# Two sides of a head's decay levels in one VectorE instruction each, and the third token tile's values on both halves of the array

## The chip, the cores and the metric

The kernel runs on one core of a Trainium2 chip. The metric is device time in microseconds, the median of the timed runs.

## What is computed

One inference step of one layer over T = 320 frames: 256 of a prompt and 64 of a running stream, D_MODEL = 1024. In order: an entry LayerNorm, one combined projection, branch A (a gated linear recurrence, HGRN2, with 8 heads of 128x128 state), branch B (a depthwise convolution), their gated mix, a LayerNorm, a mixture of 16 experts with top-2 routing, a last LayerNorm. All in float32. What matters here is branch A of one head:

```
S_t = diag(f_t) S_{t-1} + k_t v_t^T ;  o_t = S_t^T q_t
b     = cumsum(log f)                                     # per block of frames
attn  = sum_d q[t,d] k[s,d] exp(b[t,d] - b[s,d])          # for s <= t
o     = attn v + (q exp(b)) S
S_new = exp(b_last) S + (k exp(b_last - b))^T v
```

## The kernel before

The frames are held as columns: a head's q, k and running sums are 128x320 (channel x frame), in three token tiles of 128, 128 and 64 frames (`TILES`).

**Levels.** exp(b[t] - b[s]) is split at an anchor between s and t, so that no exponent is positive. For half sizes hs = 64, 32, 16, 8, 4, 2, 1 (`LV`, seven levels) a stretch of 2*hs frames has a key half in front of the anchor and a query half behind it. `X[b]` holds for each level, at offset `XO[lv]`, anchor - b in the key halves and b - anchor in the query halves: 256 columns for the first level, 320 for each of the others, 2176 in all. GpSimd writes the key halves (`key_decay`, line 1515) and VectorE the query halves (`level_decay`, line 1681), each in seven instructions of 128x160 (128x128 for the first level). ScalarE takes the exponential of all of `X[b]` in one instruction (line 1214). Then GpSimd multiplies the key halves by k (`key_side`, line 1529) and VectorE the query halves by q (`query_side`, line 1694), seven instructions each again. TensorE multiplies the halves of each level, in 64x64 blocks, into the banks of `levels`; VectorE masks the blocks (1717, 1724) and folds seven into four (1728), and GpSimd adds these up in three instructions (`level_sums`, 1541 to 1543) into `hAS`, the attention weights that `prev_out` takes.

**The order of the work.** A turn handles one head and the rests of the two before it. Each engine has its own program, written out by hand, and works it in order; semaphores tie them together. There are eight turns (`head_turn`); six are in loops of two turns. Per turn:

- VectorE: `forget_in` (log f, and at line 1672 the scan that makes the running sums `hb`), mask and fold of the head before, `level_decay`, `pprev_out` (1746), `w_low` for the next head (1641), `prev_final` (1737, 1739), `query_side`, `carry_side` (1704 to 1708), `w_low` again.
- ScalarE: `forget` (1180 to 1186), key exponential, copies, then `level_exp` (1214), `tile_exp` (1222, 1224), `w_high` (1133), `v_copy` (1206 and 1207), the square of the output (1257), two DMA issues for the states (1263), and `forget` of the next head.
- TensorE: forget projection, sum of squares, levels, transposes of the keys (line 632), query projection, states, values (`cur_v`), output of the head before.
- GpSimd: `key_decay`, `level_sums` of the head before, `key_side`.

The value projection has frames as rows: for each token tile eight matmuls (one for each 128 of the 1024 inputs) with the frames as the stationary operand (128 or 64 columns) and 128 columns of weights moving. The third tile has 64 frames and takes 64 columns of the array.

After the turns come the convolution's taps on VectorE beside the gate projections on TensorE (to about 295 us), then branch outputs, mix and router, and then the experts, for which 200 MB of weights are loaded.

Of the kernel before, what the change touches and what calls it, by code (L numbers as in the profile page):

```python
# [124 lines left out]
def build(nc, a, o):  # L125
    with ExitStack() as ctx:
# [51 lines left out]
        def carve(first, *sizes):  # L178
            out, at = [], first
            for n in sizes:  # L180
# [20 lines left out]
        (hq, hk, hV, he, hw, hls, hb, heb, hqeb, hkde, hkT, hAM, hAS, hSA, hosq, hrs, hebl, _, hSst, hSo) = carve(  # L201
            0, 2 * T, 2 * T, 384, T, T, T, T, T, T, T, 384, 3 * LW, 384, P, T, T, 4, 892, 2 * P, 2 * P)
# [65 lines left out]
        names = ("f_done q_done v_done ls_ready w_ready k_ready b_ready dr_ready dl_ready E_ready q_sb ac_ready "  # L268
                 "kde_ready xr_ready xk_ready a_done am_ready as_ready qeb_ready kdec_ready kT_done kT_sb s_done sa_sb o_done "
                 "osq_ready rms_done rstd_ready rstd_exp o_out so_ready so_stored hc_dve hp_dve hc_act hp_act hc_pool hp_pool fold_ready v_sb round")  # L270
# [270 lines left out]
        def _(pe):  # L541
# [51 lines left out]

            def cur_v(i, b, first, after_rms=False):
                pe.wait_ge(wh_in[b], i * 48 + (16, 48)[b])
                if not first:
                    pe.wait_ge(h["v_sb"], 2 * i + b)
                if after_rms:
                    pe.wait_ge(h["rstd_ready"], 2 * i + b - 1)
                value_tile(b, 0)  # L600
                value_tile(b, 1)
                value_tile(b, 2).then_inc(h["v_done"], 1)

            def levels(i, b, first):

                n1 = 2 * i + b
                pe.wait_ge(h["xr_ready"], n1 + 1)
                pe.wait_ge(h["xk_ready"], n1 + 1)
                if not first:
                    pe.wait_ge(h["am_ready"], 2 * n1)  # L610
                    pe.wait_ge(h["ac_ready"], n1)
                for t, (t0, n) in enumerate(TILES):
                    bank = LEVEL_BANKS[t]
                    for lv in range(1, 8):
                        for m in range(n // BLK):
                            s0 = t0 + BLK * m
                            if lv < 7:
                                lo = ro = X[b][:, XO[lv] + s0:XO[lv] + s0 + BLK]
                            else:
                                lo, ro = hk[:, b, s0:s0 + BLK], hq[:, b, s0:s0 + BLK]  # L620
                            last = mm(ps[BLK * m:BLK * m + BLK, bank, (lv - 1) * BLK:lv * BLK], lo, ro, True, True)
                    if t < 2:
                        last = mm(ps[0:BLK, bank, LW:LW + BLK], X[b][:, t0:t0 + BLK], X[b][:, t0 + BLK:t0 + 2 * BLK], True, True)
                    if t:
                        last.then_inc(h["a_done"], 1)

            def prev_kT(i, b, first):
                pe.wait_ge(h["kdec_ready"], 2 * i + b + 1)
                if not first:
                    pe.wait_ge(h["so_ready"], 2 * i + b)  # L630
                for t, (t0, n) in enumerate(TILES):
                    last = pe.transpose(ps[0:n, 7, t * P:t * P + P], hkde[:, t0:t0 + n], ident)
                last.then_inc(h["kT_done"], 1)

            def prev_states(i, b):
                n1 = 2 * i + b
                pe.wait_ge(h["kT_sb"], n1 + 1)
                pe.wait_ge(h["v_sb"], n1 + 1)
                for t, (t0, n) in enumerate(TILES):
                    last = mm(ps[:, 7, t * P:t * P + P], hkT[0:n, t, :], hV[0:n, t, :], True, True)  # L640
                last.then_inc(h["s_done"], 1)

            def prev_out(i, b, first):
# [7 lines left out]
                pe.wait_ge(h["as_ready"], 2 * n1 + 2)  # L651
# [5 lines left out]
                mm(ps[:, 6, 256:320], hV[0:64, 2, :], hAS[0:64, 2, 0:64], False, True).then_inc(h["o_done"], 1)  # L657
# [441 lines left out]
        def _(act):  # L1099
# [22 lines left out]
            cc = Chain(act, h["hc_act"], 6)  # L1122
            pc = Chain(act, h["hp_act"], 1)
# [77 lines left out]
            def v_copy(i, b, first):  # L1201
# [4 lines left out]
                cc(act.activation(hV[:, 0:2, :], ps[:, 3, 0:256].rearrange("p (t n) -> p t n", t=2), ACT.Copy))  # L1206
                signal(act, act.activation(hV[0:64, 2, :], ps[0:64, 3, 256:384], ACT.Copy), h["v_sb"], n + 1)

            def level_exp(i, b):
# [3 lines left out]
                act.wait_ge(h["dl_ready"], n + 1)  # L1213
# [13 lines left out]
            def prev_states(i, b, first):  # L1227
# [4 lines left out]
                pc.turn(n)  # L1232
                pc(act.activation(hkT[:, 0:2, :], ps[:, 7, 0:256].rearrange("p (t n) -> p t n", t=2), ACT.Copy))
                signal(act, act.activation(hkT[0:64, 2, :], ps[0:64, 7, 256:384], ACT.Copy), h["kT_sb"], n + 1)
# [264 lines left out]
        def _(pool):  # L1499
# [3 lines left out]
            cc = Chain(pool, h["hc_pool"], 12)  # L1503
            pc = Chain(pool, h["hp_pool"], 1)

            def key_decay(i, b):

                n = 2 * i + b
                cc.turn(n)
                pool.wait_ge(h["b_ready"], n + 1)  # L1510
                for lv, hs in enumerate(LV):
                    w = SEQ if lv == 0 else T
                    xv = X[b][:, XO[lv]:XO[lv] + w].rearrange("p (m s) -> p m s", s=2 * hs)[:, :, 0:hs]
                    bv = hb[:, 0:w].rearrange("p (m s) -> p m s", s=2 * hs)
                    ins = pool.tensor_tensor(xv, bv[:, :, hs - 1:hs].to_broadcast([P, w // (2 * hs), hs]), bv[:, :, 0:hs], ALU.subtract)  # L1515
                    if lv < 6:
                        cc(ins)
                signal(pool, ins, h["dl_ready"], n + 1)

            def key_side(i, b):  # L1520

                n = 2 * i + b
                pool.wait_ge(h["E_ready"], n + 1)
                pool.wait_ge(h["k_ready"], n + 1)
                for lv, hs in enumerate(LV):
                    w = SEQ if lv == 0 else T
                    xv = X[b][:, XO[lv]:XO[lv] + w].rearrange("p (m s) -> p m s", s=2 * hs)[:, :, 0:hs]
                    kv = hk[:, b, 0:w].rearrange("p (m s) -> p m s", s=2 * hs)[:, :, 0:hs]
                    ins = pool.tensor_tensor(xv, xv, kv, ALU.mult)  # L1529
                    if lv < 6:  # L1530
                        cc(ins)
                signal(pool, ins, h["xk_ready"], n + 1)
                cc.end()

            def level_sums(i, b, first):
# [6 lines left out]
                signal(pool, pool.tensor_tensor(hAS[BLK:P, 0:2, BLK:P], hAM[BLK:P, 0:2, 0:BLK], hAM[BLK:P, 0:2, BLK:2 * BLK], ALU.add), h["as_ready"], 2 * n + 1)  # L1542
                signal(pool, pool.tensor_tensor(hAS[0:BLK, :, 0:BLK], hAM[0:BLK, :, 0:BLK], hAM[0:BLK, :, BLK:2 * BLK], ALU.add), h["as_ready"], 2 * n + 2)
# [10 lines left out]
            head_turn((0, 0), None)  # L1554
            head_turn((0, 1), (0, 0), True)
# [3 lines left out]
            with pool.Fori(1, 4) as i:  # L1559
                head_turn((i, 0), (i - 1, 1))  # L1560
                head_turn((i, 1), (i, 0))


            head_turn(None, (3, 1))

            pool.wait_ge(tlo_ready, 2 * NG)
            for c in range(1, CT):
                pool.wait_ge(conv_done, c + 1)
                ins = pool.tensor_tensor(csum, cT[:, 0, :] if c == 1 else csum, cT[:, c, :], ALU.add)
                if c < CT - 1:  # L1570
                    signal(pool, ins, h["hc_pool"], 12 * HEADS + c)
# [4 lines left out]
        def _(dve):  # L1576
# [80 lines left out]
            cc = Chain(dve, h["hc_dve"], 15)  # L1657
            pc = Chain(dve, h["hp_dve"], 1)

            def forget_in(i, b, first):  # L1660
# [8 lines left out]
                if not (first and b == 0):  # L1669
                    dve.wait_ge(h["kde_ready"], 3 * n)  # L1670
                    dve.wait_ge(h["dl_ready"], n)
                signal(dve, dve.tensor_tensor_scan(hb, reset, hls, 0.0, ALU.mult, ALU.add), h["b_ready"], n + 1)  # L1672

            def level_decay(i, b):

                n = 2 * i + b
                for lv, hs in enumerate(LV):
                    w = SEQ if lv == 0 else T
                    xv = X[b][:, XO[lv]:XO[lv] + w].rearrange("p (m s) -> p m s", s=2 * hs)
                    bv = hb[:, 0:w].rearrange("p (m s) -> p m s", s=2 * hs)  # L1680
                    ins = dve.tensor_tensor(xv[:, :, hs:2 * hs], bv[:, :, hs:2 * hs], bv[:, :, hs - 1:hs].to_broadcast([P, w // (2 * hs), hs]), ALU.subtract)  # L1681
# [4 lines left out]
            def query_side(i, b):  # L1686
                n = 2 * i + b
                dve.wait_ge(h["E_ready"], n + 1)
                dve.wait_ge(h["q_sb"], n + 1)
                for lv, hs in enumerate(LV):  # L1690
                    w = SEQ if lv == 0 else T
                    xv = X[b][:, XO[lv]:XO[lv] + w].rearrange("p (m s) -> p m s", s=2 * hs)[:, :, hs:2 * hs]
                    qv = hq[:, b, 0:w].rearrange("p (m s) -> p m s", s=2 * hs)[:, :, hs:2 * hs]
                    ins = dve.tensor_tensor(xv, xv, qv, ALU.mult)  # L1694
# [16 lines left out]
            def level_mask(i, b, first):  # L1711
                n = 2 * i + b
                dve.wait_ge(h["a_done"], 2 * n + 1)
                if not first:
                    dve.wait_ge(h["as_ready"], 2 * n - 1)
# [3 lines left out]
            def last_mask(i, b, first):  # L1719
                n = 2 * i + b  # L1720
                dve.wait_ge(h["a_done"], 2 * n + 2)
                if not first:
                    dve.wait_ge(h["as_ready"], 2 * n)
# [24 lines left out]
            def head_turn(cur, nxt, prev, pprev, first=False, first_prev=False):  # L1748
# [16 lines left out]
                query_side(*cur)  # L1765
# [496 lines left out]
```

## Time and profile before

| | |
|---|---|
| median of 3 runs | 856.8 us (855.72 to 857.4) |
| span of the profiled execution | 854.3 us |
| PE busy | 812.5 us, 95% |
| DVE busy | 423.0 us, 50%, 706 instructions |
| ACT busy | 239.4 us, 28%, 378 instructions |
| POOL (GpSimd) busy | 84.0 us, 10%, 146 instructions |
| HBM traffic | 293 GB/s over the span |

The span is that of one execution taken by the hardware profiler, from the first to the last instruction; it has no other time of its own on the page. The timed median is 2.5 us over it. The page's busy shares are means over stages with different limits.

### The profile page before, as it was taken

How to read it: one execution, taken by the hardware profiler on the slowest of the kernel's cores; microseconds unless marked ns; L12 is line 12 of the kernel's file. 1: busy time of each engine (PE TensorE's matmuls, PEld its weight loads, DVE VectorE, ACT ScalarE, POOL GpSimd, SP SyncE). 2: the span in 40 equal slices, each digit the busy share in tenths (PEclk: the TensorE clock that was granted, in tenths of full speed). 3: DMA queues.
4: the chain of work that ended last, by engine and by line, in shares of the span. 5: the costliest groups of instructions: out<-in, count | busy, mean ns of one | idle time of the engine just before them, and what ended most of it. 6: DMA issues, size and time to landing. Idle time of an engine off the chain costs nothing.

```text
span 854.3 us, 12979 instructions
## 1 busy us (share of the span) xinstructions
PE 812.5 (95%) x5068; PEld 525.6 (62%) x5068; DVE 423.0 (50%) x706; ACT 239.4 (28%) x378; POOL 84.0 (10%) x146
## 2 busy tenths in 40 slices
PE   4999999999999999999999999999999999999892
PEld 2988888999999976576353453534435344352261
DVE  6788888988999993786010201202012021120137
ACT  5656666564454426102102010000100001000011
POOL 1354445530000100000000000000000000000000
PEclk9999999999999999999999999999999999999996
DMA  8422222234444844578999999999999999999991
GB/s 315 171 84 85 83 83 83 107 125 161 148 148 147 320 172 143 229 289 340 425 411 407 429 427 430 424 427 427 428 423 427 427 428 428 428 422 426 429 390 64
DMA packets 33883, 251.16 MB, mean 294 GB/s; under 512 B 4974, under 2 KB 8430, under 8 KB 21674
## 3 DMA queue, kind: packets, MB, share of 16 engines
q1 hardware_dynamic: 31296, 249.18, 71.9%
q10 hardware_dynamic: 2538, 1.32, 0.5%
q8 instruction: 33, 0.54, 0.2%
q14 instruction: 16, 0.13, 0.0%
HBM read 247.99 MB, written 2.48 MB: 293 GB/s over the span
## 4 chain that ended last, share of the span: by engine, by line
PE 57%; DVE 21%; DMA 9%; ACT 9%; issue 2%; ACTq 1%; DVEq 0%; SPq 0%
PE ps L543 56%; DMA ring<-in_w_up_e 8%; DVE ar L1803 5%; DVE ring L1681 4%; DVE split_t L1810 3%; ACT ring L1214 2%; ACT ar L1224 1%; DVE ar L1717 1%; ACT split_w L1133 1%; DVE ar L1728 1%; PE ps L942 1%; DVE ar L1672 1%; ACTq L1263 1%; ACT ar L1186 1%; DMA ring<-in_w_in 1%
## 5 line engine op out<-in xcount | busy, mean ns | idle before, releaser
L543 PE MATMUL ps<-ring,ar 128*64 128x512 f32 (+1 forms) x976 | 202.0, 567 | 1.1 <-DMA ring<-in_w_up_e 1.1
L543 PE MATMUL ps<-ring,xT 128*64 128x512 f32 (+2 forms) x848 | 149.5, 451 | 4.6 <-DMA ring<-in_w_gate_e 3.0
L543 PEld LDWEIGHTS ps<-ring,ar 128*64 128x64 f32 x976 | 68.0, 137 | 120.3 <-issue 112.5
L543 PEld LDWEIGHTS ps<-ring,xT 128*64 128x64 f32 (+1 forms) x848 | 75.2, 153 | 71.7 <-issue 62.7
L543 PE MATMUL ps<-split_x,split_t 128*128 128x320 f32 x672 | 101.0, 310 | 0.5 <-DVE split_t L1810 0.5
L543 PEld LDWEIGHTS ps<-split_x,split_t 128*128 128x128 f32 x672 | 98.6, 188 | 2.5 <-issue 0.8
L2113 DVE TENSOR_TENSOR ar<-ar,ps 128x512 f32<-128x512 f32 (+1 forms) x42 | 28.8, 685 | 134.5 <-PE ps L543 132.7
L543 PE MATMUL ps<-split_x,split_w 128*128 128x320 f32 x480 | 80.7, 324 | 3.3 <-ACT split_x L1165 1.0
L543 PEld LDWEIGHTS ps<-split_x,split_w 128*128 128x128 f32 x480 | 74.1, 196 | 6.5 <-ACT split_x L1168 2.1
L1803 DVE SCALAR_TENSOR_TENSOR ar<-ar,params 128x350 f32<-128x350 f32 x116 | 68.7, 592 | 4.1
L543 PE MATMUL ps<-ar 128*64 128x512 f32 (+7 forms) x424 | 66.7, 342 | 2.9 <-DVE mid L1746 2.9
L2080 DVE SCALAR_TENSOR_TENSOR out_lo<-ps,ar,out_hi 128x1024 fp32r<-128x1024 f32 x7 | 9.0, 1284 | 104.6 <-ACT out_hi L1434 104.6
L543 PEld LDWEIGHTS ps<-ar 128*64 128x64 f32 (+3 forms) x424 | 39.6, 152 | 25.4 <-issue 22.9
L543 PEld LDWEIGHTS ps<-ar,mid 128*128 128x128 f32 x384 | 43.6, 192 | 8.3 <-issue 7.3
L543 PE MATMUL ps<-ar,mid 128*128 128x128 f32 x384 | 45.5, 278 | 0.2 <-DVE ar L2068 0.2
L543 PE MATMUL ps<-mid,ring 128*128 128x320 f32 x128 | 34.9, 432 | 0.0
L1515 POOL TENSOR_TENSOR ring<-ar 128x160 f32<-128x160 f32 (+1 forms) x56 | 28.2, 503 | 63.3 <-DVE ar L1672 59.5
L1434 ACT ACTIVATE out_hi<-ps,ar 128x1024 fp32r<-128x1024 f32 x7 | 7.8, 1114 | 94.2 <-PE ps L543 94.2
L2094 DVE TENSOR_TENSOR ar<-ar,ps 128x1024 f32<-128x1024 f32 x7 | 8.5, 1221 | 51.7 <-PE ps L543 51.7
L1417 ACT ACTIVATE ar<-ps 128x1024 f32<-128x1024 f32 x8 | 8.2, 1026 | 88.5 <-PE ps L543 88.4
L1529 POOL TENSOR_TENSOR ring<-ring,ar 128x160 f32<-128x160 f32 (+1 forms) x56 | 30.4, 542 | 25.1 <-ACT ring L1214 16.0
L1694 DVE TENSOR_TENSOR ring<-ring,ar 128x160 f32<-128x160 f32 (+1 forms) x56 | 30.4, 543 | 2.1 <-ACT ring L1214 0.2
(233 smaller groups left out, 860.9 us busy)
## 6 DMA issues: line engine op xcount, KB each, us to landing
ring<-in_w_gate_e SPq DMA_DIRECT2D x29, 2048.0 KB, 21.0
ring<-in_w_up_e SPq DMA_DIRECT2D x29, 2048.0 KB, 17.4
ring<-in_w_down_e SPq DMA_DIRECT2D x22, 2048.0 KB, 17.3
ring<-in_w_in SPq DMA_DIRECT2D x56, 512.0 KB, 4.5
ar<-in_w_down_e SPq DMA_DIRECT2D x4, 1792.0 KB, 18.7
ring<-in_w_down_end SPq DMA_DIRECT2D x3, 2048.0 KB, 35.3
ar<-in_w_up_e SPq DMA_DIRECT2D x3, 1792.0 KB, 14.5
ring<-in_w_o_a SPq DMA_DIRECT2D x8, 512.0 KB, 5.4
```

What stands on the lines that cost most here:

```text
L543: return pe.matmul(out, lhsT, rhs, start=start, stop=stop)
L942: last = pe.transpose(ps[:, k // 4, (k % 4) * P:(k % 4) * P + P], eh[:, k * P:k * P + P], ident)
L1133: signal(act, act.activation(piece(wh, q), sh[:, b, q].rearrange("p k n -> p (k n)"), ACT.Copy), whi_ready, 2 * n + q + 1)
L1214: signal(act, act.activation(X[b], X[b], ACT.Exp), h["E_ready"], n + 1)
L1515: ins = pool.tensor_tensor(xv, bv[:, :, hs - 1:hs].to_broadcast([P, w // (2 * hs), hs]), bv[:, :, 0:hs], ALU.subtract)
L1529: ins = pool.tensor_tensor(xv, xv, kv, ALU.mult)
L1681: ins = dve.tensor_tensor(xv[:, :, hs:2 * hs], bv[:, :, hs:2 * hs], bv[:, :, hs - 1:hs].to_broadcast([P, w // (2 * hs), hs]), ALU.subtract)
L1694: ins = dve.tensor_tensor(xv, xv, qv, ALU.mult)
L1803: vc(dve.scalar_tensor_tensor(acc, uc[:, c, j:j + CW], vt[:, c, j:j + 1], acc, ALU.mult, ALU.add))
L1810: signal(dve, dve.tensor_tensor(t_lo[1 - b][q][1], stl[:, b, 8 * q:8 * q + 8].rearrange("p k n -> p (k n)"), t_hi[1 - b][q][0], ALU.subtract),
L2080: signal(dve, dve.scalar_tensor_tensor(out_lo[:, :], ps[:, 6:8, :].rearrange("p b n -> p (b n)"), gs, hiF, ALU.mult, ALU.subtract), e["eos ...
L2113: signal(dve, dve.tensor_tensor(yv, yv, ps[0:c, 4 + j % 2, :], ALU.add), e["y_added"], 6 * n + j + 1 + 6 * late)
```

## The change

Four edits.

1. VectorE writes both sides of a level in one instruction. It needs -b beside b, so the negated sums `hnb` are laid in front of `hb`, by one new instruction after the scan; `both_sums` is a view whose first half lies in `hnb` (key halves) and whose second half, T + hs further, lies in `hb` (query halves), and `anchors` is the anchor of each. The multiplication does the same with `hk` laid in front of `hq` (`key_query`). The seven instructions of `level_decay` and the seven of the multiplication now have 320 columns (256 for the first level); GpSimd's fourteen are gone with the semaphores around them, and it keeps `level_sums`.
2. The values of the third token tile are computed in two halves of the array: even inputs k into rows 0 to 63, odd ones into rows 64 to 127 of PSUM. The two partial sums are never added: the keys and attention weights that meet them are held twice, in both halves.
3. For that the third tile's key transpose becomes two matmuls against the identity (one for each half), and `level_sums` has a fourth instruction, which writes the third tile's weights into rows 64 to 127.
4. ScalarE's `v_copy` and the copy of the transposed keys are one instruction of 128x384 each, in place of 128x256 and 64x128.

```diff
+        (hk, hq, hV, he, hw, hls, hnb, hb, heb, ...) = carve(...)
+        NB_AT = 4 * T + 384 + 3 * T
+        def key_query(b, hs, w):
+            v = ar[:, b * T:b * T + 2 * (2 * T + hs)].rearrange("p (j t) -> p j t", j=2)[:, :, 0:w]
+            return v.rearrange("p j (m s) -> p m j s", s=2 * hs)[:, :, :, 0:hs]
+        def both_sums(hs, w):
+            v = ar[:, NB_AT:NB_AT + 2 * (T + hs)].rearrange("p (j t) -> p j t", j=2)[:, :, 0:w]
+            return v.rearrange("p j (m s) -> p m j s", s=2 * hs)[:, :, :, 0:hs]
+        def anchors(hs, w):
+            v = ar[:, NB_AT:NB_AT + 2 * T].rearrange("p (j t) -> p j t", j=2)[:, :, 0:w]
+            return v.rearrange("p j (m s) -> p m j s", s=2 * hs)[:, :, :, hs - 1:hs].to_broadcast([P, w // (2 * hs), 2, hs])
...
+            def value_halves(b):
+                for k in range(KT):
+                    side = 64 * (k % 2)
+                    last = mm(ps[side:side + 64, 3, 2 * P:3 * P], xT[:, k, SEQ:T], sh[:, b, 3, k, :], k < 2, k >= KT - 2)
+                return last
...
-                value_tile(b, 2).then_inc(h["v_done"], 1)
+                value_halves(b).then_inc(h["v_done"], 1)
...
-                for t, (t0, n) in enumerate(TILES):
-                    last = pe.transpose(ps[0:n, 7, t * P:t * P + P], hkde[:, t0:t0 + n], ident)
+                for t in range(2):
+                    pe.transpose(ps[:, 7, t * P:t * P + P], hkde[:, t * P:t * P + P], ident)
+                for side in (0, 64):
+                    last = mm(ps[side:side + 64, 7, 2 * P:3 * P], hkde[:, SEQ:T], ident, True, True)
...
-                cc(act.activation(hV[:, 0:2, :], ps[:, 3, 0:256].rearrange("p (t n) -> p t n", t=2), ACT.Copy))
-                signal(act, act.activation(hV[0:64, 2, :], ps[0:64, 3, 256:384], ACT.Copy), h["v_sb"], n + 1)
+                signal(act, act.activation(hV, ps[:, 3, 0:384].rearrange("p (t n) -> p t n", t=3), ACT.Copy), h["v_sb"], n + 1)
...
-            def head_turn(cur, prev, first_prev=False):
-                if cur:
-                    key_decay(*cur)
-                if prev:
-                    level_sums(*prev, first_prev)
-                if cur:
-                    key_side(*cur)
...
+                signal(pool, pool.tensor_tensor(hAS[BLK:P, 2, 0:BLK], hAM[0:BLK, 2, 0:BLK], hAM[0:BLK, 2, BLK:2 * BLK], ALU.add), h["as_ready"], 3 * n + 3)
...
                 signal(dve, dve.tensor_tensor_scan(hb, reset, hls, 0.0, ALU.mult, ALU.add), h["b_ready"], n + 1)
+                cc(dve.tensor_scalar(hnb, hb, -1.0, None, ALU.mult))
...
-                    ins = dve.tensor_tensor(xv[:, :, hs:2 * hs], bv[:, :, hs:2 * hs], bv[:, :, hs - 1:hs].to_broadcast([P, w // (2 * hs), hs]), ALU.subtract)
+                    ins = dve.tensor_tensor(xv, both_sums(hs, w), anchors(hs, w), ALU.subtract)
...
-                    ins = dve.tensor_tensor(xv, xv, qv, ALU.mult)
+                    ins = dve.tensor_tensor(xv, xv, key_query(b, hs, w), ALU.mult)
```

## Rows read from the trace of the kernel before

**Rows 1.** Page: shares of the chain that ended last, by engine.
```profile
PE 57%; DVE 21%; DMA 9%; ACT 9%; issue 2%; ACTq 1%; DVEq 0%; SPq 0%
```
**Rows 2.** Busy time by stretch: window, us, engines, clock, DMA share, GB/s.
```profile
65.00:165.00 100.00, 96.52 (x958) 89.27 (x958) 87.17 (x147) 63.73 (x117) 47.30 (x85) 1.00 0.28 94
200.00:295.00 95.00, 94.71 (x638) 93.19 (x636) 88.92 (x136) 48.34 (x59) 0.00 (x0) 1.00 0.49 177
295.00:854.00 559.00, 535.38 (x2758) 264.29 (x2757) 166.18 (x288) 68.13 (x103) 3.06 (x3) 0.99 0.90 373
```
**Rows 3.** Chain of waits: start, us, what; scans of the third and eighth turns.
```profile
65.30 0.84 DVE ar L1672
...
164.63 0.84 DVE ar L1672
```
**Rows 4.** Timeline of DVE: start, us, what; second, sixth and eighth turns.
```profile
46.57 1.09 DVE L1717 TENSOR_TENSOR ar<-ps,mid 128x896 f32<-128x896 f32 x1 [0.49 <-PE ps L543]
...
128.89 0.76 DVE L1728 TENSOR_TENSOR ar<-ar 128x576 f32<-128x576 f32 x1
129.68 4.15 DVE L1681 TENSOR_TENSOR ring<-ar 128x128 f32<-128x128 f32 x7
...
136.94 3.90 DVE L1694 TENSOR_TENSOR ring<-ring,ar 128x128 f32<-128x128 f32 x7
...
143.91 0.49 DVE L1664 SCALAR_TENSOR_TENSOR ar<-ps,ar 128x320 f32<-128x320 f32 x1 [0.31 <-ACT ar L1186]
...
167.26 0.88 DVE L1728 TENSOR_TENSOR ar<-ar 128x576 f32<-128x576 f32 x1
168.18 4.15 DVE L1681 TENSOR_TENSOR ring<-ar 128x128 f32<-128x128 f32 x7
```
**Rows 5.** Timeline of ACT, 133 to 142 us.
```profile
133.91 2.02 ACT L1214 ACTIVATE ring<-ring 128x2176 f32<-128x2176 f32 x1 [4.64 <-DVE ring L1681]
...
138.81 0.38 ACT L1206 ACTIVATE ar<-ps 128x256 f32<-128x256 f32 x1
139.22 0.27 ACT L1207 ACTIVATE ar<-ps 64x128 f32<-64x128 f32 x1
139.53 0.44 ACT L1257 ACTIVATE ar<-ps 128x320 f32<-128x320 f32 x1
...
141.19 0.44 ACT L1180 ACTIVATE ar<-ps 128x320 f32<-128x320 f32 x1 [1.22 <-issue]
```
**Rows 6.** Timeline of PE: two stretches of levels, values, output.
```profile
121.04 0.92 PE L543 MATMUL ps<-ring 128*64 128x64 f32 x24
...
122.84 0.98 PE L543 MATMUL ps<-ring 128*64 128x64 f32 x14
...
128.73 5.73 PE L543 MATMUL ps<-ring,xT 128*128 128x128 f32 x48
134.89 1.44 PE L543 MATMUL ps<-ar 128*128 128x128 f32 x10 [0.43 <-DVE mid L1746]
```
**Rows 7.** Groups of DVE by line and shape: busy, mean ns.
```profile
L1707 DVE TENSOR_TENSOR ar<-ar 128x320 f32<-128x320 f32 x8 | 3.9, 492 | 0.3
...
L1883 DVE TENSOR_SCALAR ar<-cst 128x128 f32<-128x128 f32 x1 | 0.2, 228 | 0.0
L1969 DVE TENSOR_SCALAR ar<-cst 128x12 f32<-128x12 f32 x1 | 0.2, 166 | 0.0
```
**Rows 8.** Chain of waits, last instructions of the sixth turn's level_decay.
```profile
131.24 1.05 DVE ring L1681
...
132.31 0.51 DVE ring L1681
...
132.84 0.64 DVE ring L1681
...
133.50 0.34 DVE ring L1681
```
**Rows 9.** Timeline of POOL, the first of that turn's level sums.
```profile
131.10 0.99 POOL L1541 TENSOR_TENSOR ar<-ar 128x384 f32<-128x384 f32 x1
```

More of the change, by code:

```diff
@@ L199, in build @@
         sgu = sgu_f.rearrange("p (b n) -> p b n", b=2)
-        (hq, hk, hV, he, hw, hls, hb, heb, hqeb, hkde, hkT, hAM, hAS, hSA, hosq, hrs, hebl, _, hSst, hSo) = carve(
-            0, 2 * T, 2 * T, 384, T, T, T, T, T, T, T, 384, 3 * LW, 384, P, T, T, 4, 892, 2 * P, 2 * P)
+        (hk, hq, hV, he, hw, hls, hnb, hb, heb, hqeb, hkde, hkT, hAM, hAS, hSA, hosq, hrs, hebl, _, hSst, hSo) = carve(
+            0, 2 * T, 2 * T, 384, T, T, T, T, T, T, T, T, 384, 3 * LW, 384, P, T, T, 4, 892 - T, 2 * P, 2 * P)
+        NB_AT = 4 * T + 384 + 3 * T
[8 more added lines that the diff above has]
+            return v.rearrange("p j (m s) -> p m j s", s=2 * hs)[:, :, :, hs - 1:hs].to_broadcast([P, w // (2 * hs), 2, hs])
         two = lambda v: v.rearrange("p (b n) -> p b n", b=2)
@@ L267, in build @@
         st_in = [sem(f"st_in{b}") for b in range(2)]
-        names = ("f_done q_done v_done ls_ready w_ready k_ready b_ready dr_ready dl_ready E_ready q_sb ac_ready "
-                 "kde_ready xr_ready xk_ready a_done am_ready as_ready qeb_ready kdec_ready kT_done kT_sb s_done sa_sb o_done "
-                 "osq_ready rms_done rstd_ready rstd_exp o_out so_ready so_stored hc_dve hp_dve hc_act hp_act hc_pool hp_pool fold_ready v_sb round")
+        names = ("f_done q_done v_done ls_ready w_ready k_ready b_ready dr_ready E_ready q_sb ac_ready "
+                 "kde_ready xr_ready a_done am_ready as_ready qeb_ready kdec_ready kT_done kT_sb s_done sa_sb o_done "
+                 "osq_ready rms_done rstd_ready rstd_exp o_out so_ready so_stored hc_dve hp_dve hc_act hc_pool hp_pool fold_ready v_sb round")
         h = {n: sem(n) for n in names.split()}
@@ L639, in prev_states @@
                 for t, (t0, n) in enumerate(TILES):
-                    last = mm(ps[:, 7, t * P:t * P + P], hkT[0:n, t, :], hV[0:n, t, :], True, True)
+                    last = mm(ps[:, 7, t * P:t * P + P], hkT[:, t, :], hV[:, t, :], True, True)
                 last.then_inc(h["s_done"], 1)
@@ L650, in prev_out @@
                 pe.wait_ge(h["sa_sb"], n1 + 1)
-                pe.wait_ge(h["as_ready"], 2 * n1 + 2)
+                pe.wait_ge(h["as_ready"], 3 * n1 + 3)
                 pe.wait_ge(h["ac_ready"], n1 + 1)
@@ L1231, in prev_states @@
                     act.wait_ge(h["s_done"], n)
-                pc.turn(n)
-                pc(act.activation(hkT[:, 0:2, :], ps[:, 7, 0:256].rearrange("p (t n) -> p t n", t=2), ACT.Copy))
-                signal(act, act.activation(hkT[0:64, 2, :], ps[0:64, 7, 256:384], ACT.Copy), h["kT_sb"], n + 1)
+                signal(act, act.activation(hkT, ps[:, 7, 0:384].rearrange("p (t n) -> p t n", t=3), ACT.Copy), h["kT_sb"], n + 1)
             def prev_cross(i, b, first):
@@ L1502, in _ @@
             signal(pool, pool.tensor_tensor(piece(wl, 0), sh[:, 0, 0].rearrange("p k n -> p (k n)"), piece(whF, 0), ALU.subtract), wlo_ready, 1)
-            cc = Chain(pool, h["hc_pool"], 12)
             pc = Chain(pool, h["hp_pool"], 1)
[L1506 to L1533, printed above, removed]
             def level_sums(i, b, first):
@@ L1541, in level_sums @@
                 pc(pool.tensor_tensor(hAM[:, :, 0:2 * BLK], hAM[:, :, 0:2 * BLK], hAM[:, :, 2 * BLK:4 * BLK], ALU.add))
-                signal(pool, pool.tensor_tensor(hAS[BLK:P, 0:2, BLK:P], hAM[BLK:P, 0:2, 0:BLK], hAM[BLK:P, 0:2, BLK:2 * BLK], ALU.add), h["as_ready"], 2 * n + 1)
-                signal(pool, pool.tensor_tensor(hAS[0:BLK, :, 0:BLK], hAM[0:BLK, :, 0:BLK], hAM[0:BLK, :, BLK:2 * BLK], ALU.add), h["as_ready"], 2 * n + 2)
+                signal(pool, pool.tensor_tensor(hAS[BLK:P, 0:2, BLK:P], hAM[BLK:P, 0:2, 0:BLK], hAM[BLK:P, 0:2, BLK:2 * BLK], ALU.add), h["as_ready"], 3 * n + 1)
+                signal(pool, pool.tensor_tensor(hAS[0:BLK, :, 0:BLK], hAM[0:BLK, :, 0:BLK], hAM[0:BLK, :, BLK:2 * BLK], ALU.add), h["as_ready"], 3 * n + 2)
+                signal(pool, pool.tensor_tensor(hAS[BLK:P, 2, 0:BLK], hAM[0:BLK, 2, 0:BLK], hAM[0:BLK, 2, BLK:2 * BLK], ALU.add), h["as_ready"], 3 * n + 3)
                 pc.end()
-            def head_turn(cur, prev, first_prev=False):
-                if cur:
-                    key_decay(*cur)
-                if prev:
-                    level_sums(*prev, first_prev)
-                if cur:
-                    key_side(*cur)
-            head_turn((0, 0), None)
-            head_turn((0, 1), (0, 0), True)
+            level_sums(0, 0, True)
             pool.wait_ge(router_in, 32)
@@ L1559, in _ @@
             with pool.Fori(1, 4) as i:
-                head_turn((i, 0), (i - 1, 1))
-                head_turn((i, 1), (i, 0))
-            head_turn(None, (3, 1))
+                level_sums(i - 1, 1, False)
+                level_sums(i, 0, False)
+            level_sums(3, 1, False)
             pool.wait_ge(tlo_ready, 2 * NG)
@@ L1570, in _ @@
                 if c < CT - 1:
-                    signal(pool, ins, h["hc_pool"], 12 * HEADS + c)
+                    signal(pool, ins, h["hc_pool"], c)
             ins.then_inc(csum_ready, 1)
@@ L1656, in _ @@
             signal(dve, dve.memset(hrs, 0.0), h["o_out"], 1)
-            cc = Chain(dve, h["hc_dve"], 15)
+            cc = Chain(dve, h["hc_dve"], 16)
             pc = Chain(dve, h["hp_dve"], 1)
@@ L1684, in level_decay, with both_sides @@
                 signal(dve, ins, h["dr_ready"], n + 1)
-            def query_side(i, b):
+            def both_sides(i, b):
                 n = 2 * i + b
@@ L1714, in level_mask @@
                 if not first:
-                    dve.wait_ge(h["as_ready"], 2 * n - 1)
+                    dve.wait_ge(h["as_ready"], 3 * n)
                 wide = mask.rearrange("p (o n) -> p o n", o=1).to_broadcast([P, 2, LW])
@@ L1722, in last_mask @@
                 if not first:
[L1723 removed]
+                    dve.wait_ge(h["as_ready"], 3 * n)
                 signal(dve, dve.tensor_tensor(hAM[0:BLK, 2, :], ps[0:BLK, LEVEL_BANKS[2], 0:LW], mask[0:BLK, :], ALU.mult), h["am_ready"], 2 * n + 2)
@@ L1764, in head_turn @@
                     w_low(*nxt, 1)
-                query_side(*cur)
+                both_sides(*cur)
                 carry_side(*cur, first)
```

15 lines of the change are left out of this document (5 added, 10 removed).

## The prediction

> **What bounds the kernel now.** I read the shares of the chain first [rows 1]: TensorE carries 57% and VectorE 21%, so the bound changes by stage. Busy time by stretch shows where [rows 2]. From 295 us on the experts keep TensorE (535 of 559 us) and the DMAs (0.90) full and VectorE idle; nothing of the change lies there. From 200 to 295 us VectorE and TensorE are both nearly full, with no instruction touched. The change lies in the eight head turns, 31 to 180 us: TensorE is 97% busy, VectorE 87%, GpSimd 47%, so which engine ends a turn has to be read from waits.
>
> A turn is 19.9 us: five lie between the scans at 65.30 and 164.63 us [rows 3]. In the timeline of one turn [rows 4] VectorE ends `level_decay` at 133.83; ScalarE, idle for 4.64 us until then, starts its exponential at 133.91 [rows 5] and works without a hole through `tile_exp`, `w_high`, `v_copy`, the square, the DMA issues and `forget` of the next head, for whose last result VectorE waits 0.31 us at 143.91 [rows 4]. Then VectorE again: `forget_in`, scan, masks, fold, `level_decay`. That is the loop: 9.8 us on VectorE, 10 us on ScalarE. Beside it VectorE alone comes within 0.31 us of a full turn, and TensorE within 0.43 us, waiting for `pprev_out` (line 1746), which stands right behind `level_decay` [rows 6]. So a time counts in full if it lies between w_ready and the end of `level_decay` on VectorE or between `level_exp` and `forget` on ScalarE. The rest of VectorE counts once its small slack is used, and TensorE's saving only if the loop gets shorter.
>
> **The change, part by part.**
>
> *The negated sums.* One instruction between scan and mask, on the loop. A tensor_scalar with a constant took 0.166 us for 12 columns and 0.228 for 128 [rows 7], 0.53 ns for a column, so 0.33 for 320, and 0.03 for the gap: +0.37 a turn. Bounds: 0.23 (128 columns) and 0.49, what a tensor_tensor of 320 columns takes.
>
> *level_decay, alone.* 320 columns of tensor_tensor are 0.49 us [rows 7] and 160 are 0.34 [rows 8] (the last one there), so 256 are 0.43. One of 0.43, six of 0.49 and the gaps of 0.02 make 3.5 to 3.6; I take 3.57. Alone, seven of the old ones would make 2.5. The doubled instructions are cheaper than two, but the other half of that work was on GpSimd.
>
> *level_decay beside level_sums.* What hid it before was partly paid for: old instructions took 1.05, 0.51 and 0.64 us where one with nothing beside it took 0.34 [rows 8]. The first of them meets GpSimd's sum of 128x384 at 131.10 [rows 9]: VectorE is held for 1.05 - 0.34 = 0.71, then 0.17 and 0.30 by the two small sums. This doesn't go away. `level_sums` is released by the fold, right in front of `level_decay`, and with `key_decay` gone GpSimd is free to start it at once, so all sums fall into the seven instructions: 0.71 + 0.17 + 0.30, and about 0.10 for the new fourth one (64x64, an estimate from the 0.17 of 64x128) = 1.28. The block of seven becomes 3.57 + 1.28 = 4.85. The fold is freed from `key_decay` and takes 0.76. From the fold's start to the end of `level_decay` before: 4.94 at 128.89 and 5.07 at 167.26 [rows 4], the smallest and largest of the seven turns that have a fold, mean 5.00. After: 0.79 + 4.85 = 5.64. So +0.64 a turn. Bounds: -0.64 if no sum holds VectorE, +0.92 if the wide sum holds it for its whole 0.99 [rows 9] in place of 0.71.
>
> The Trainium skill ("SBUF — State Buffer", Who interferes with whom) says that a VectorE instruction with two SBUF inputs and a GpSimd instruction that reads SBUF exclude each other, the later one blocked for the whole of the other. Here the 0.99 us sum held VectorE 0.71, not 0.99. By the whole duration the block would be larger by 0.28 us a turn, some 2 us in all, about 864.5; the sum goes by the measured hold.
>
> *The multiplication.* 3.90 before [rows 4], with GpSimd beside it throughout; 3.57 with GpSimd idle: -0.33, on VectorE's side branch. All of VectorE's turn grows by 0.37 + 0.64 - 0.33 = 0.68, the loop by more (below), so VectorE's slack goes from 0.31 to about 0.4 and it stays behind the loop. GpSimd's fourteen instructions were not on the loop, but for the first turn.
>
> *v_copy.* 0.38 + 0.27 and a gap of 0.03 each [rows 5] become one of 384 columns. 256 columns took 0.38 and 320 took 0.44, so 384 take 0.49, with the gap 0.51 for 0.72: -0.21, on the loop. The same saving on the transposed keys lies in ScalarE's 4.64 us of idle time: nothing.
>
> *Third value tile.* 24 matmuls took 5.73 us [rows 6], so eight are 1.9. In the levels 12 matmuls that alternate between the halves of the array took some 0.75 us (121.04 to the next group), seven of the lone third tile 0.82 (122.84 on): 62 against 117 ns each. At that ratio the eight take 1.0, so TensorE saves 0.9 a turn. It waited 0.43 for `pprev_out` already; the saving makes that wait longer. Worth nothing (at most 0.9 a turn, were TensorE the bound). The two identity matmuls in place of a transpose add some 0.1, hidden likewise, but for the last turn: behind it TensorE works without a hole for 17 us, so +0.1 once.
>
> *Sum.* A turn: +0.37 + 0.64 - 0.21 = +0.80; six turns (third to eighth): 4.8. The second turn's mask waits 0.49 for TensorE's levels [rows 4], which hides its own negation; but that TensorE work starts behind the first turn's `level_decay` and low parts, later by the first turn's negation: +0.4, + 0.64 - 0.21 = 0.83. With the 0.1 at the end 5.7. The following stages are full and start that much later. 854.3 + 5.7 = 860.0 for the span; the median of the runs stands 2.5 over the profiled span, so **862.5 us**.
>
> **The rivals.**
>
> *The stride costs.* For hs = 1 the new views jump between `hnb` and `hb` at every column. No row of before shows VectorE reading so. Were its data phase twice as long, one of seven would take 0.33 more: eight turns of `level_decay` are +2.6, and the multiplications another 0.33 on the side branch, still inside its slack. Time: about 865. For hs = 2 the same would double it, 867.7, the upper end. The Trainium skill ("SBUF — State Buffer", Door 1: The DMA port swizzle) states that an access pays for each change of a 16-byte line unless two accesses fall into it; by that hs = 1 pays and hs = 2 doesn't. No run here shows it.
>
> *GpSimd doesn't get in (the other side).* Place: the gap of 0.02 us between two VectorE instructions. If GpSimd's sums wait until the seven are through, `level_decay` and fold take 3.57 + 0.79 = 4.36, so 0.64 less, and a turn changes by 0.37 - 0.64 - 0.21 = -0.48: seven turns are -3.3, time about 853.5. It decides from the point where the four sums hold VectorE less than 0.8 us a turn in place of 1.28. Against it: in every turn before, GpSimd's wide sum did get in (1.05 us at 131.24). For it: the sums could also be shorter in their hold once nothing else queues.
>
> *The halves don't overlap* (the change doesn't do what it says): TensorE's eight matmuls keep their 1.9 us. TensorE's own turn stays 19.5 us against a loop of 20.7: same 862.5.
>
> *The delay is absorbed.* If the experts' stage were set by transfers that don't start later, the 5.7 us would come back: 857. Against it: loads wait for places that earlier stages free.
>
> **How the numbers follow.** The main case (with the halves either way) 0.52, stride 0.25, GpSimd locked out or the holds small 0.14, absorbed 0.06, something worse 0.03. Likeliest 862.5; its own range 860 to 864.5 from the bounds of negation and holds. The range to give is 857 to 867: it leaves out the faster case and little above. Within 0.2% means 855.1 to 858.5, about what a measurement of this kernel can tell from no change. Slower: main, stride and the worse case, 0.80; same: 0.07; faster: 0.13.
>
> **What would show it.** In the changed trace: a tensor_scalar of 0.33 us behind each scan; `level_decay` of about 4.85 us, in which the second instruction takes about 1.2, and of 3.57 in the first turn; the multiplication 3.57 with equal instructions of 0.49; one ScalarE copy of 0.49; scans 20.7 us apart in place of 19.9; TensorE's wait for `pprev_out` above 1 us; TensorE's values 4.8 us in place of 5.7. An hs = 1 instruction (the seventh) of 0.8 is the stride case. A second instruction of 0.49 is the case of GpSimd locked out. Scans under 20 us apart with the rows as forecast would mean that I have the wrong loop.

## The result, and the profile after

| | before | after |
|---|---|---|
| median | 856.56 us (4 runs, 855.72 to 857.4) | 862.53 us (4 runs, 860.67 to 866.9) |
| ratio | | 1.0083, 95% interval 1.0066 to 1.010 |
| profiled execution: span, granted clock | 854.3 us, 0.992 | 865.0 us, 0.981 (time 866.9) |
| GpSimd busy | 84.0 us | 31.7 us |
| third to eighth scan, per turn | 19.87 us | 20.95 us |

The change makes the kernel 0.8% slower, some 6 us, clear of the noise; the forecast was 862.5. The four executions are of two kinds: two of 860.7 us with a mean granted clock of 0.987 and 0.989, and 864.3 and 866.9 at 0.981 to 0.982. The profiled one is the slowest of them. (Time and span of one execution differ by 1.9 us: 866.9 and 865.0 here, and 856.2 in a later execution of the kernel before whose span was 854.3 too. So 1.9 us lie around a span, not 2.5.)

The VectorE and GpSimd timelines of the sixth turn after, against [rows 4, 9]:

```profile
132.44 0.82 DVE L1650 TENSOR_TENSOR_SCAN ar<-cst,ar 128x320 f32<-128x320 f32 x1
133.30 0.33 DVE L1651 TENSOR_SCALAR ar<-ar 128x320 f32<-128x320 f32 x1
...
135.75 0.76 DVE L1706 TENSOR_TENSOR ar<-ar 128x576 f32<-128x576 f32 x1
136.54 4.75 DVE L1659 TENSOR_TENSOR ring<-ar 128x256 f32<-128x256 f32 x7
```
```profile
136.59 1.23 POOL L1530 TENSOR_TENSOR ar<-ar 128x384 f32<-128x384 f32 x1 [19.14 <-DVE ar L1706]
...
139.37 0.45 POOL L1533 TENSOR_TENSOR ar<-ar 64x64 f32<-64x64 f32 x1
```

`level_decay` has grown from 4.15 to 4.75 us. The chain of waits shows its seven instructions one by one, against [rows 8]:

```profile
136.54 0.44 DVE ring L1659
...
137.00 1.18 DVE ring L1659
...
138.21 0.65 DVE ring L1659
...
138.87 0.78 DVE ring L1659
...
139.67 0.50 DVE ring L1659
...
140.20 0.50 DVE ring L1659
...
140.73 0.58 DVE ring L1659
```

An instruction with nothing beside it takes 0.50 (the fifth and sixth). The second is held 0.68 us by the wide sum, the third 0.15, the fourth 0.28, the fifth not at all. The wide sum's 1.23 us start 0.41 before the second instruction does, so only its last 0.82 us lie beside it. The last, hs = 1, takes 0.08 more than its neighbours.

These holds are not new. Before, the sums held the same stretch of VectorE for 0.71 + 0.17 + 0.30 us [rows 8], and its first instructions were longer too while GpSimd's `key_decay` ran beside them (0.54 and 0.51 us for 160 columns, against 0.34 alone):

```profile
129.68 0.44 DVE ring L1681
...
130.14 0.54 DVE ring L1681
...
130.70 0.51 DVE ring L1681
```

So of the 4.15 us before some 2.5 were its own work and 1.65 lay in holding; of the 4.75 after, 3.66 are its own work (e2_late_sums, below) and 1.09 holding. The block grew by the half that GpSimd had done, not by the sums.

The multiplication (line 1672), the joined copy (line 1229) and the negation (line 1651) by groups:

```profile
L1672 DVE TENSOR_TENSOR ring<-ring,ar 128x320 f32<-128x320 f32 x48 | 24.3, 506 | 1.6
...
L1651 DVE TENSOR_SCALAR ar<-ar 128x320 f32<-128x320 f32 x8 | 2.6, 327 | 0.3
```
```profile
L1229 ACT ACTIVATE ar<-ps 128x384 f32<-128x384 f32 x8 | 3.9, 492 | 0.3
```

What the forecast did not have is in TensorE's timeline of the turn before this one, against [rows 6]. The first two lines are an undisturbed turn, the output matmuls and the forget projection:

```profile
99.10 1.30 PE L559 MATMUL ps<-ar 128*128 128x128 f32 x10 [1.54 <-DVE mid L1724]
100.21 3.76 PE L559 MATMUL ps<-split_x,split_w 128*128 128x320 f32 x24
...
112.77 4.76 PE L559 MATMUL ps<-ring,xT 128*128 128x128 f32 x48
120.09 2.37 PE L559 MATMUL ps<-ar 128*128 128x128 f32 x10 [2.56 <-DVE mid L1724]
122.22 5.62 PE L559 MATMUL ps<-split_x,split_w 128*128 128x320 f32 x24
```

The values take 4.76 us in place of 5.73, then TensorE waits 2.56 us for `pprev_out`, and behind that wait the output matmuls (ten records) take 2.37 us in place of 1.30 (1.44 before) and the forget projection 5.62 in place of 3.76: the granted clock is at its lower level, 0.50 or half of the full one, from 120 to 126 us. `forget` on ScalarE then waits for TensorE, and VectorE's wait for `forget` is 2.16 us. This turn took 22.45 us. The same happened, for a shorter time, behind a wait of 2.49 us (output matmuls 1.91, forget projection 4.77), and not behind those of 1.54 and 1.53. A third drop lies ahead of the third scan and so outside the mean of the turns: behind a wait of 2.18 us the second turn's forget and query projections take 8.85 us, against 7.31 before.

```profile
37.31 8.85 PE ps L559 x48
```

### The profile page after: what moved, and what is told of

It reads as the page before. It is cut to its first block, busy times and chain, and to the rows that moved or that the text cites. A ratio compares the mean times of both kernels' runs of the same rounds, so it can differ in the third digit from the quotient of the medians.

```text
span 865.0 us, 12835 instructions
## 1 busy us (share of the span) xinstructions
PE 812.2 (94%) x5092; PEld 525.3 (61%) x5092; DVE 426.4 (49%) x714; ACT 236.6 (27%) x362; POOL 31.7 (4%) x42
## 3 DMA queue, kind: packets, MB, share of 16 engines
q10 hardware_dynamic: 2538, 1.32, 0.5%
## 4 chain that ended last, share of the span: by engine, by line
PE 60%; DVE 22%; DMA 8%; ACT 7%; issue 2%; ACTq 0%; DVEq 0%
PE ps L559 58%; DMA ring<-in_w_up_e 8%; DVE ar L1781 6%; DVE ring L1659 4%; DVE split_t L1788 3%; ACT ring L1235 1%; DVE ar L1695 1%; PE ps L966 1%; ACT ar L1245 1%; DVE ar L1650 1%; DVE ar L1706 1%; ACT split_w L1156 1%; ACT ar L1209 1%; DVE ring L1569 1%; DVE ar L1702 1%
## 5 line engine op out<-in xcount | busy, mean ns | idle before, releaser
L559 PE MATMUL ps<-ring,xT 128*64 128x512 f32 (+2 forms) x848 | 141.8, 451 | 4.6 <-DMA ring<-in_w_gate_e 3.0
L559 PEld LDWEIGHTS ps<-ring,xT 128*64 128x64 f32 (+1 forms) x848 | 68.3, 153 | 70.8 <-issue 62.6
L559 PE MATMUL ps<-split_x,split_w 128*128 128x320 f32 x480 | 85.0, 336 | 6.1 <-DVE split_w L1620 3.5
L559 PEld LDWEIGHTS ps<-split_x,split_w 128*128 128x128 f32 x480 | 78.5, 207 | 10.2 <-DVE split_w L1620 3.9
L559 PE MATMUL ps<-ar 128*64 128x512 f32 (+5 forms) x424 | 65.7, 345 | 11.0 <-DVE mid L1724 11.0
L559 PEld LDWEIGHTS ps<-ar 128*64 128x64 f32 (+2 forms) x424 | 40.0, 158 | 32.1 <-issue 31.1
L1659 DVE TENSOR_TENSOR ring<-ar 128x320 f32<-128x320 f32 (+1 forms) x56 | 35.4, 632 | 1.9
L1175 ACT ACTIVATE split_t<-ring 128x1024 fp32r<-128x1024 f32 x24 | 25.5, 1061 | 20.3 <-DMA ring<-in_w_in 11.6
L559 PEld LDWEIGHTS ps<-mid,ring 128*128 128x128 f32 x128 | 24.3, 190 | 10.1
```

What stands on the lines that cost most here:

```text
L559: return pe.matmul(out, lhsT, rhs, start=start, stop=stop)
L1175: signal(act, act.activation(t_hi[1 - b][q][1], stl[:, b, 8 * q:8 * q + 8].rearrange("p k n -> p (k n)"), ACT.Copy), thi_ready, 2 * n + q + 1)
L1659: ins = dve.tensor_tensor(xv, both_sums(hs, w), anchors(hs, w), ALU.subtract)
```

## The experiments

One table first. Times are medians. The runs were spread over several chips of the same kind; each ratio is to the kernel before on the same chip, whose median was between 855.7 and 856.4, with its 95% interval. "Turn" is a fifth of the time from the third to the eighth scan in the profile.

| kernel | median us (lowest to highest) | ratio to before | turn us |
|---|---|---|---|
| before (time beside e1 to e4, turn of the profile before) | 855.74 | | 19.87 |
| changed, again (a1_after) | 865.01 (863.33 to 866.22) | 1.0093 (1.0078 to 1.0109) | 20.94 |
| e1_series | 863.66 (862.37 to 863.68) | 1.0087 (1.0074 to 1.0100) | 20.47 |
| e2_late_sums | 880.46 (877.0 to 881.59) | 1.0275 (1.0255 to 1.0295) | 23.39 |
| e3_mult_only | 855.86 (854.49 to 857.13) | 0.9998 (0.9989 to 1.0007) | 19.66 |
| e4_halves_only | 856.24 (854.07 to 860.58) | 1.0003 (0.9989 to 1.0017) | 19.72 |
| e5_no_negation | not comparable | | 20.33 |
| e6_short_sum | not comparable | | 19.83 |
| e7_filler | 862.75 (862.52 to 863.85) | 1.0075 (1.0061 to 1.0088) | 20.50 |
| e8_mult_filler | 855.32 (853.65 to 856.51) | 0.9984 (0.9975 to 0.9993) | 19.66 |
| e9_late_filler | 866.09 (865.82 to 866.58) | 1.0110 (1.0095 to 1.0124) | 21.02 |
| e10_double_negation | 866.20 (864.88 to 867.6) | 1.0121 (1.0103 to 1.0140) | 20.86 |

**Where TensorE's clock comes in.** The changed kernel once more:

> The changed kernel once more, for its spread beside the others. Theory A (six undisturbed turns of 20.5 us and, by chance, some turns with the clock at half behind TensorE's wait): 860.5 in executions without such turns, up to 867 with them, median 862.5. Rival: all at 862 to 863.

It came out at 865.01, all six executions between 863.3 and 866.2, with mean clocks of 0.975 to 0.985: neither the 860.5 and the median of 862.5 that I expected nor the rival's 862 to 863. The one that was profiled has the same three drops as the first profile, behind waits of 2.25, 2.40 and 2.56 us. Then the order of the third tile's matmuls:

```diff
-                for k in range(KT):
+                for k in (0, 2, 4, 6, 1, 3, 5, 7):
                     side = 64 * (k % 2)
```

> The changed kernel with the eight value matmuls of the third token tile in another order: the four of the first half of the array, then the four of the second, in place of alternating. Same results, same instructions. Theory A (the loop over VectorE and ScalarE sets the turn, and TensorE's clock drop in the profile after comes from its long wait for pprev_out, which the halves make longer): the values take about 5.7 us a turn again in place of 4.76, TensorE's wait for pprev_out falls from 1.5 to 0.6 us or so, the granted clock stays at 1.00 through the turns, and the time is 860 to 861 with little spread. Rival B (the clock drops have nothing to do with the wait): waits shorter, drops as before, time 862 to 863. Rival C (TensorE is a bound after all): 0.9 us a turn more, 868 or above.

A weak test: the values took 5.25 us, not 5.7, so only half a microsecond of TensorE's wait was filled; waits of 1.8 and 2.1 us stayed, and no drop stands in the profile's head turns (span 860.5, third scan at 66.24 in place of 67.85). Its median of 863.66 misses the forecast of 860 to 861, mostly because I wrote spans where times were meant; by the time alone rival B's 862 to 863 lies nearer. The strong test fills the wait with work that nobody reads:

```diff
                 value_tile(b, 1)
+                for _ in range(6):
+                    mm(ps[:, 3, 3 * P:4 * P], ident, ident, True, True)
                 value_halves(b)
```

> The changed kernel with six more matmuls of 128x128 per turn, into columns of the values' bank that nobody reads, between the second and third token tile's values; 1.4 us of TensorE work in the time in which it waits for pprev_out. Theory A (the saved TensorE time turns into a wait, behind which the clock falls): the wait falls from 1.5-2.5 to some 0.5 us, the granted clock stays at 1.00 through the turns, and the time is 860.5 with a spread under 1 us although TensorE does more. Rival (drops come anyway): median 862.5 and the same spread. If TensorE were the bound: 871.

TensorE does 1.4 us more a turn, and the kernel is 2.3 us faster than the unfilled one on the same chip (862.75 against 865.01; five of six executions within 0.3 us). The forecast of 860.5 was again a span (it is 860.7), and the waits are 1.0 to 1.2 us, not 0.5. Busy time by stretch of the changed kernel (its first profile) and of this one, columns as in [rows 2]:

```profile
60.00:110.00 50.00, 44.85 (x489) 41.11 (x488) 41.68 (x72) 30.66 (x54) 5.89 (x8) 0.97 0.32 106
110.00:150.00 40.00, 35.71 (x357) 33.48 (x356) 33.58 (x57) 22.00 (x39) 5.90 (x8) 0.91 0.23 76
```
```profile
60.00:110.00 50.00, 46.88 (x518) 43.24 (x519) 41.98 (x71) 30.88 (x54) 5.89 (x8) 1.00 0.29 102
110.00:150.00 40.00, 37.57 (x404) 34.69 (x402) 35.15 (x60) 24.00 (x42) 5.89 (x8) 1.00 0.26 88
```

The granted clock (third column from the end) goes from 0.97 and 0.91 to 1.00, and the turn from 20.95 to 20.50. So the drops in the head turns added 2.3 us in the median on this chip.

The filled kernel is still 6.4 us of span behind the kernel before, and not all of that is there at full clock. At 385.93 us it is 4.5 late (the same VectorE instruction started at 381.44 before). Then matmuls of the router's stage take longer than the same ones before; first before, second filled:

```profile
392.48 6.17 PE L543 MATMUL ps<-mid,cst 128*128 128x512 f32 x14
```
```profile
398.89 8.08 PE L559 MATMUL ps<-mid,cst 128*128 128x512 f32 x14
```

From 396 to 403 us its granted clock is 0.52, and at 443.13 us (before 436.48) it is 6.65 late. The profile of the kernel before has no such stretch there; those of all the changed versions have one, of some 3 to 7 us, between 389 and 421 us. What brings it on is open: the wait in front of it is 0.41 us. So the change costs 4.5 us at full clock, and with the 1.9 around a span that makes 860.7 us, the time of the two fastest executions on the first chip. The profiled one of 866.9 had some 4 more from the three drops in its head turns and some 2 from the one behind 385 us.

**The negation.** Left out:

```diff
-                cc(dve.tensor_scalar(hnb, hb, -1.0, None, ALU.mult))
```

(`hnb` is set to zero once at the start instead.)

> The changed kernel without the negated sums: the instruction behind each scan is left out and the negated half holds zeros, so the key sides of the levels are wrong; all else stays. Theory A (the negation lies on the loop for its whole length): 0.36 us a turn less, 2.5 to 3 in all: 858 to 859 in executions of equal clock. Rival (it was hidden by the mask's wait for TensorE): no difference to the changed kernel.

The attention weights are others now, and the passes for tokens that an expert's first pass does not take (the late passes) ran: 2,924 us, with 13,892 matmuls in place of 5,092. Only its head turns can be read. Two of them had the clock down (0.91 and 0.92 in their stretches, without a filler), so the mean of 20.33 is blurred; the last two took 19.98 and 19.49 us against 20.31 and 19.82 with the negation in e1_series, 0.33 less each. So I doubled it, on top of the filler, with unchanged results:

```diff
                 cc(dve.tensor_scalar(hnb, hb, -1.0, None, ALU.mult))
+                cc(dve.tensor_scalar(hnb, hb, -1.0, None, ALU.mult))
```

> The changed kernel with the six filler matmuls (the one that took 862.75), and the negation behind each scan done twice. Theory A (the negation lies on the loop for its whole length): 0.36 us more in each turn from the third, so scans 20.86 us apart in place of 20.50, some 2.5 to 2.9 in all, 865.5. Rival (part of it is hidden by other waits): under 1 us more.

20.86 a turn against 20.50, both at full clock: +0.36, what was forecast. The negation lies on the loop for its whole length. In time the difference is 3.4 us (866.20 against 862.75, on different chips) where 2.5 to 2.9 were forecast; its four executions are two of 864.9 and two of 867.5, and the profiled spans differ by 2.4.

**The sums' hold.** The wide sum cut from 384 to 12 columns (the rest of that sum is left out):

```diff
-                pc(pool.tensor_tensor(hAM[:, :, 0:2 * BLK], hAM[:, :, 0:2 * BLK], hAM[:, :, 2 * BLK:4 * BLK], ALU.add))
+                pc(pool.tensor_tensor(hAM[:, :, 0:4], hAM[:, :, 0:4], hAM[:, :, 2 * BLK:2 * BLK + 4], ALU.add))
```

> The changed kernel with GpSimd's wide level sum cut from 128x384 to 128x12 (the rest of that sum is left out, so the attention weights are wrong). Theory A (the sum holds VectorE's doubled second instruction for 0.67 us, on the loop): level_decay 4.75 to about 4.15, 0.6 a turn less, 4 to 4.5 in all: 856.5 to 858. Rival (VectorE pays for the wider views, not for GpSimd): level_decay stays at 4.75.

The late passes ran here too (2,916 us), and the turns tell it (clock 1.00 in all of them):

```profile
129.43 4.07 DVE L1659 TENSOR_TENSOR ring<-ar 128x256 f32<-128x256 f32 x7
```

4.07 in place of 4.75, and 19.83 us a turn against 20.50 with the filler: 0.68 and 0.67. The wide sum's length costs VectorE that, and the loop passes on all of it. That shows what a hold on the loop is worth; it is not a cost that the change brought, since the same sum held VectorE 0.71 us before.

**Moving the sums.** They wait for the end of `level_decay`:

```diff
                 pool.wait_ge(h["fold_ready"], n + 1)
+                if late:
+                    pool.wait_ge(h["dr_ready"], n + 2)
```

> The changed kernel with GpSimd's level sums held until the seven instructions of level_decay are through (one more wait, on the semaphore of their end); the last head's sums as before. Theory A (the sums hold VectorE's doubled instructions for 1.1 us a turn, on the loop): level_decay falls from 4.75 to 3.66 us. The sums then end some 2.3 us behind level_decay and TensorE's output matmuls start behind them, 1.3 us later than after pprev_out; of that about 0.9 is slack before ScalarE's forget. Net -0.7 a turn, 857 to 859; but the longer wait may lower the clock more often, which would give up to 862. Rival B (the hold is no cost of the loop): level_decay 3.66 and the time at or above 862.

`level_decay` did fall to 3.66 us, and the kernel took 880. This was my largest miss. GpSimd's and TensorE's timelines:

```profile
124.50 1.00 POOL L1532 TENSOR_TENSOR ar<-ar 128x384 f32<-128x384 f32 x1 [20.23 <-DVE ring L1661]
125.58 1.32 POOL L1533 TENSOR_TENSOR ar<-ar 64x128 f32<-64x128 f32 x1
126.98 0.58 POOL L1534 TENSOR_TENSOR ar<-ar 64x192 f32<-64x192 f32 x1
127.63 0.54 POOL L1535 TENSOR_TENSOR ar<-ar 64x64 f32<-64x64 f32 x1
```
```profile
128.23 2.39 PE L559 MATMUL ps<-ar 128*128 128x128 f32 x10 [3.27 <-POOL ar L1535]
130.38 5.39 PE L559 MATMUL ps<-split_x,split_w 128*128 128x320 f32 x24
```

The blocking works the other way here: the sum of 64x128, 0.59 us after the change, takes 1.32 in every turn with VectorE's `w_low` beside it (1.39 us at 125.19, 1.22 after the change). The sums end 3.8 us behind `level_decay`, not 2.3; TensorE waits 3.27 for them, and what follows runs at the lower clock. To part the two, the same kernel with twelve filler matmuls:

> The changed kernel with late level sums (the one that took 880) and twelve more matmuls of 128x128 per turn in TensorE's wait. Theory A (of its 18 us over the changed kernel a part is the chain sums, output matmuls, forget projection, and a part is that chain run at half clock behind a wait of 3.3 us): the output and forget projection take 1.4 and 3.8 us again in place of 2.4 and 5.4, and the time is 866 to 870. Rival (the clock adds nothing): 880.

```profile
121.56 1.33 PE L559 MATMUL ps<-ar 128*128 128x128 f32 x10 [0.61 <-POOL ar L1537]
122.70 3.76 PE L559 MATMUL ps<-split_x,split_w 128*128 128x320 f32 x24
```

866.09 and 21.02 a turn. Over the kernel before on their own chips the late sums cost 24.7 us, the late sums with fillers 9.7 and the change with fillers 6.5. So of some 18 us that the late sums had cost against the filled kernel about 15 were the clock, and 3 the new chain over GpSimd and TensorE, although VectorE saves 1.1 a turn.

**Half of the change.** The subtraction shared with GpSimd again (no negation), the multiplication on VectorE alone, halves and joined copies kept. Of this edit only VectorE's line is shown; GpSimd's seven subtractions and their semaphore come back with it:

```diff
-                    ins = dve.tensor_tensor(xv, both_sums(hs, w), anchors(hs, w), ALU.subtract)
+                    ins = dve.tensor_tensor(xv[:, :, hs:2 * hs], bv[:, :, hs:2 * hs], bv[:, :, hs - 1:hs].to_broadcast([P, w // (2 * hs), hs]), ALU.subtract)
```

> The changed kernel with level_decay as before the change: GpSimd subtracts the key halves again (seven instructions), VectorE the query halves, no negated sums. The multiplication stays on VectorE alone with 320 columns, and the halves and the joined copies stay. Theory A: the loop loses 0.37 (negation) and 0.6 (doubled level_decay beside the sums), and keeps -0.21 of v_copy: 855 to 856 if the clock holds, at or just under the kernel before. Rival B (the doubled multiplication or the halves cost the time): 860 or above.

19.66 us a turn and 855.86: the whole loss is gone with the merged subtraction and its negation. Taking the multiplication back too, so that only halves and joined copies are left:

> Only the third token tile's halves, the two matmuls against the identity, the fourth sum and the joined copies; subtraction and multiplication shared by GpSimd and VectorE as before the change. Theory A: v_copy gives 0.21 a turn, TensorE's saving only lengthens its wait: 855 to 857, with a granted clock that drops in some turns if waits of 1.3 us and more do that. Rival B (TensorE was part of the bound): 850 or below.

19.72 a turn, 856.24: no difference to the kernel before that can be told, and a wider spread (854.07 to 860.58). TensorE's 0.9 us a turn shows nowhere: the turn is 0.15 shorter, no more than the joined copy was to give. Last, the first of these two with five filler matmuls:

> The kernel with the subtraction shared by GpSimd and VectorE again and the rest as changed (the one that took 855.9), with five more matmuls of 128x128 per turn into unread columns. Theory A (turns of 19.66 us against 19.87 before the change, and some clock drops behind longer waits): the drops vanish and the time is 854.5, 1 to 1.5 under the kernel before. Rival: 856 or above, TensorE being full.

855.32 against 856.37 beside it, ratio 0.9984 (0.9975 to 0.9993), the one version that beats both kernels. That is between the forecast of 854.5 and the rival's 856. How much of that the fillers bring is not settled: e3_mult_only has the same turn, its profile has a mean clock of 0.89 before 60 us and 1.00 from there to 206, its span is 853.9 against 853.1, and the two were timed on different chips.

## Why the prediction was right, point by point

- **The loop** [rows 3 to 5]: right. Two terms moved by experiment, the negation (+0.36) and the wide sum (-0.68), came out in the turn at 0.36 and 0.67.
- **Negation** +0.37: measured 0.33 and the gap.
- **level_decay and fold** +0.64: 0.76 + 0.03 + 4.75 = 5.54 against 5.00, so +0.54. The mechanism was right to the instruction (second 1.18, about 1.2 forecast). Two sizes were off: the holds sum to 1.11, not 1.28 (the fourth sum holds nothing that shows), and hs = 1 takes 0.08 more.
- **v_copy** -0.21: 0.49 as forecast.
- **Multiplication**: 3.66 in place of 3.57, off the loop as said; VectorE's waits for `forget` ahead of the sixth and seventh scans are 0.33 and 0.36 us in e1_series at full clock, against 0.34 and 0.31 before and 0.4 forecast.
- **Sum per turn** +0.80: +0.63 at full clock (20.50 against 19.87); the terms as measured would make +0.69. The filled kernel is 4.2 us late at the eighth scan, 4.8 at the last fold and 4.6 at a group of 128x512 matmuls much later (357.14 against 352.52), so nothing is absorbed up to there. The 5.7 of the forecast is 4.5 at 385 us.
- **Third value tile**: 0.97 us saved on TensorE (0.9 forecast), worth nothing, and its wait is longer: right. That the longer wait costs was missing. I priced it at nothing, since a wait in front of an engine that isn't the bound is free; but the granted clock fell behind three of the waits in the profiled execution, and in the turn of 22.45 us `forget`, and with it VectorE, waited for TensorE. This is the step that failed: the drops cost some 4 us there, and 2.3 in the median against the filled kernel.
- **From span to time** +2.5: it is 1.9.

So the hit to 0.03 us is luck, though the loop and its direction were right: 5.7 was 1.2 too much, 2.5 was 0.6 too much, and the clock, which the forecast did not have, put 1.8 back in the median (0 to 6 in an execution).

The rivals: stride, right in kind and a quarter of its size (0.08 for 0.33). GpSimd locked out: wrong, in the turns read it gets in after the first VectorE instruction (second instruction 1.18). Halves that don't overlap: wrong, 4.76 us. Absorption: wrong; what follows the head turns even took some 2 us longer in the filled kernel, in the stretch at the lower clock from 396 to 403 us. No experiment looked at that stage, so whether the change brings the stretch on is not shown.

## What to carry to other kernels

Work shared between VectorE and GpSimd should be priced by what is beside it afterwards: here each merged instruction was cheaper than two, but GpSimd's half had been done beside the loop and now lies on it (3.66 us for some 2.5), the sums hold VectorE about as long as before (1.09 us for 1.18), and a helper instruction (the negation, 0.36) came with the merge. A saving on an engine that waits is not worth nothing: if it lengthens a wait until TensorE's clock falls, it is a loss, and matmuls that nobody reads can be a gain (2.3 us here). Before moving a GpSimd instruction, look at both engines' neighbours: the block acts in both directions.

## What was not expected of the hardware

- Behind TensorE waits of 2.49, 2.56 and 3.27 us the next 3 to 7 us ran at the lower granted clock (24 matmuls in 4.77, 5.62 and 5.39 us for 3.8). The length of the wait alone does not decide. The clock fell too behind 2.03 (e3_mult_only) and 2.04 us (e5_no_negation); it stayed at 1.00 behind 2.13 (e1_series) and, in the second turn, behind 2.54 (e2_late_sums) and 2.55 us (e6_short_sum). Here are the 48 matmuls behind the wait of 2.54 us; behind the 2.18 us of the changed kernel the same ones took 8.85:

```profile
36.48 7.31 PE ps L559 x48
```

- The eight value matmuls of 64 columns took 1.9 us of TensorE one after the other, 0.97 less when they alternated between the halves of the array, and 0.48 less when four on one half were followed by four on the other (values 5.73, 4.76 and 5.25 us).
- A GpSimd sum of 128x384 that took 0.99 to 1.24 us held a VectorE instruction with two SBUF inputs 0.67 to 0.71 us. A VectorE instruction of 1.39 us stretched a GpSimd sum of 64x128 from 0.59 to 1.32.
- A tensor_tensor whose input jumps between two regions at every column took 0.57 to 0.58 us for 320 columns; at every second column or more 0.50.
